# Rotary halves of the second pair: a swap by transfers inside SBUF in place of a product with a sign matrix

## The chip, the cores and the metric

The kernel runs on one core of one Trainium2 chip. The metric is device time in microseconds (us) of one execution, and what stands for a kernel is the median of its runs. Before the change the runs gave a median of 1918.45 us (1917.8 to 1918.78, three runs).

## What is computed

Two blocks of two layers each, in fp32, on 512 tokens of width 1024. The first block ("first pair" of layers below) has windowed attention, a Fourier mix and a short convolution. The second block ("second pair") is the one that the change touches. Each of its layers has three kinds of attention side by side (a: 6 heads with a dilated mixture, b: 4 heads of differential attention, c: 6 heads with latent queries and keys), a projection, a layer norm and a gated feed-forward part. The change is in kind c:

```python
q = (rms_norm(c_q, q_norm_g) @ w_uq).reshape(Bn, S, C_HEADS, C_NOPE + C_ROPE)     # 6 heads, 64 + 32
kv = (rms_norm(c_kv, kv_norm_g) @ w_ukv).reshape(Bn, S, C_HEADS, C_NOPE + C_V)
q_c = concat([q[..., :C_NOPE], apply_rope(q[..., C_NOPE:])])
k_c = concat([kv[..., :C_NOPE], broadcast(apply_rope(k_r))])                      # one rotary k for all heads

def apply_rope(x):                      # half = 16, angles of S = 512 positions
    x1, x2 = x[..., :half], x[..., half:]
    return concat([x1 * cos - x2 * sin, x2 * cos + x1 * sin])
```

So each group of 32 rotary values needs its own two halves of 16 swapped, one of them with its sign turned.

## The kernel before, in words

*Layout.* Activations stand with features on the 128 partitions and the 512 tokens along the row. `qr` holds the rotary part: `qr[:, 0, :]` the queries of heads 0 to 3 (4 x 32 partitions), `qr[0:64, 1, :]` those of heads 4 and 5, and `qr[64:96, 1, :]` the common rotary key. A swap of halves is then a swap of neighbouring blocks of 16 partitions. The kernel gets it from TensorE: `rot` is a 128x128 matrix of 0, 1 and -1, and `rot` times `qr` is the swapped and signed copy, in PSUM (`turn_rope`, line 1947). In the first pair the kernel does the same swap in another way: SyncE issues 16 transfers from SBUF to SBUF per layer, each of 16 partitions (lines 696 to 701), and the sign is in the table `sin1`.

*Weights.* Every weight tile comes into one of three slots of `raw` by a transfer that SyncE issues in the order of the list `stream`; it waits until GpSimd has finished with the tile that was three places ahead (line 708, 744). ScalarE copies it to `w_hi` (line 847), GpSimd subtracts to get `w_lo` (line 775), and TensorE makes three products for each one (`mm3`, lines 1411 to 1413). `w_hi` and `w_lo` have two slots. In a layer of the second pair the order of tiles is c, bq, bk, bv, a, av, up, then the four tiles of the output projection ("o",0,0), ("o",0,1), ("o",1,0), ("o",1,1), then the feed-forward tiles.

*The stretch of the change*, once in each layer l, y = 2 + l. Each engine follows an order written out by hand, and engines wait for each other by semaphores.

- TensorE: the av projection with eight early scores of kind b among it; then from the tile up: two groups of `qr` (lines 1945, 1946), three products for the key part `kn` with the two products of `rot` behind the second and the third one (line 1963), three for `qn`, two scores of kind b (units 8 and 9), four products for `vc`; then score(10), the first of kind c (line 1999), and the loop of the attention stage (from line 2001) with scores, transposes and products with the values. A score of kind c waits for `s_roped`, for the rotary key, and for the last `qn` copy (lines 1907 to 1909).
- ScalarE copies each result out of PSUM: the rotary key (line 1302), `qr` (line 1306, with the query scale in it), `kn` and `qn` (line 1311), `vc` (line 1315), then the exponentials (line 1290).
- VectorE, when the early scores are done, for both groups (lines 2623 to 2630): a product with `sin2` into `tmp_c`, a product with `cos2` in `qr`, and for each of the six heads the sum into `qc`. Behind that stand the first `scored` steps of the attention stage (line 2599).
- GpSimd, when the second group's product with `cos2` is done: the sum for the key of head 0 into `kc` (line 820) and five copies of it (line 823).
- SyncE has at this place the wait and the load for tile ("o",1,0).

PSUM banks: the two products of `rot` use banks 5 and 7 (`ROTB`), and the next user of each waits for the sums of its group (`emptied`). `tmp_c` lies in the same memory as the attention output `ao`; it is free in this stretch.

Of the kernel before, what the change touches and what calls it, by code (L numbers as in the profile page):

```python
# [16 lines left out]
ALU = mybir.AluOpType  # L17
# [3 lines left out]
P = 128  # L21
D = 1024
KD = D // P
SEQ, CTX, DEPTH = 512, 256, 2
# [19 lines left out]
QC = HD + ROPE  # L44
# [27 lines left out]
def _constants():  # L72

    f = np.float32
    c = {}
    c["ident"] = np.eye(P, dtype=f)
    pos = np.arange(SEQ)
    inv = np.power(f(10000.0), -np.arange(16, dtype=f) / f(16)).astype(f)
    ang = np.stack([(pos // 64).astype(f)[:, None] * inv, (pos % 64).astype(f)[:, None] * inv], 1)
    rows = np.arange(P)  # L80
    axis, freq = (rows % 64) // 32, rows % 16
    c["cos1"] = np.ascontiguousarray(np.cos(ang)[:, axis, freq].T.astype(f))
    sign = np.where(rows % 32 < 16, -1.0, 1.0).astype(f)[:, None]
    c["sin1"] = np.ascontiguousarray(np.sin(ang)[:, axis, freq].T.astype(f) * sign)

    def rotation(n, half):
        r = np.zeros((n, n), f)
        for i in range(n):
            first = (i % (2 * half)) < half
            r[i + half if first else i - half, i] = -1.0 if first else 1.0  # L90
        return r

    c["rot"] = rotation(P, 16)
    inv2 = np.power(f(10000.0), -np.arange(16, dtype=f) / f(16)).astype(f)
    ang2 = pos.astype(f)[:, None] * inv2
    c["cos2"] = np.ascontiguousarray(np.tile(np.cos(ang2).T, (P // 16, 1)).astype(f))
    c["sin2"] = np.ascontiguousarray(np.tile(np.sin(ang2).T, (P // 16, 1)).astype(f))
    q, k = np.arange(P)[:, None], np.arange(3 * P)[None, :] - P
    band = np.where(np.abs(q - k) <= P, 0.0, FAR).astype(f)
    c["band_mid"] = np.concatenate([np.zeros((P, CTX), f), band], 1)  # L100
    c["band_first"] = np.concatenate([np.zeros((P, CTX), f), band[:, P:]], 1)
    for n in (SEQ, CTX):
        t = np.outer(np.arange(n), np.arange(n)) % n * (2 * np.pi / n)
        c[f"dft{n}"] = np.concatenate([np.cos(t)[:, 0:n // 2 + 1], np.sin(t)[:, 1:n // 2]], 1).astype(f) / f(np.sqrt(n))
    t = np.outer(np.arange(HD), np.arange(HD)) % HD * (2 * np.pi / HD)
    two = np.eye(2)
    c["dft_ccos"] = np.kron(two, np.cos(t) / 8.0).astype(f)
    c["dft_csin"] = np.kron(two, -np.sin(t) / 8.0).astype(f)
    dist = SEQ - 1 - np.arange(SEQ + P)
    df = np.maximum(dist, 1).astype(f)  # L110
    large = 16 + (np.log(df / f(16)) / f(np.log(2048 / 16)) * f(16)).astype(np.int32)
    bucket = np.where(dist < 16, np.maximum(dist, 0), np.minimum(large, BUCKETS - 1))
    hot = np.zeros((BUCKETS + 2, SEQ + P), f)
    hot[bucket, np.arange(SEQ + P)] = (dist >= 0)
    times = (dist <= P).astype(int) + (dist % 4 == 0) + (dist % 16 == 0)
    ok = dist >= 0
    hot[BUCKETS] = np.where(ok & (times > 0), np.log(np.maximum(times, 1)), -FAR)
    hot[BUCKETS + 1] = np.where(ok, 0.0, -FAR)
    c["hot"] = hot
    pick = np.zeros((2, A_HEADS + B_HEADS), f)  # L120
    pick[0, :A_HEADS] = 1.0
    pick[1, A_HEADS:] = 1.0
    c["pick"] = pick
    fold = np.zeros((P, 2), f)
    for g in range(4):
        fold[32 * g:32 * g + 2] = np.eye(2, dtype=f)
    c["fold"] = fold
    d2 = 384 + np.arange(P)[:, None] - np.arange(SEQ)[None, :]
    c["causal"] = np.where(d2 >= 0, 0.0, FAR).astype(f)
    init = [0.8 - 0.6 * np.exp(-0.3 * l) for l in range(DEPTH)]  # L130
    c["lam_init"] = np.array([[-i, 1.0 - i] for i in init], f)
    return c


def _program(nc, I, out, seen):
    ctx = ExitStack()
    with ctx:
# [23 lines left out]
        rot = put("rot", [P, P])  # L161
# [84 lines left out]
        qr = at("qr", [P, 2, SEQ], names["g_hi"][0] + 4 * C_HEADS * SEQ)  # L246
# [3 lines left out]
        tmp_c = at("tmp_c", [P, 2, SEQ], ao2_at)  # L250
# [14 lines left out]
        sin2 = put("sin2", [P, SEQ])  # L265
# [26 lines left out]
        ps = ctx.enter_context(nc.psum_tensor("ps", [P, 8, 512], F32))  # L292
# [57 lines left out]
        s_proj = Signal(nc, ctx, seen, "proj")  # L350
# [9 lines left out]
        s_row_stored = Signal(nc, ctx, seen, "row_stored")  # L360
        s_sum_cols = Signal(nc, ctx, seen, "sum_cols")
        s_roped = Signal(nc, ctx, seen, "roped")
        s_rot = Signal(nc, ctx, seen, "rot")
        s_rot_in = Signal(nc, ctx, seen, "rot_in")
        s_rr = Signal(nc, ctx, seen, "rr")
        s_rr_mm = Signal(nc, ctx, seen, "rr_mm")
        s_scored = Signal(nc, ctx, seen, "scored")
# [6 lines left out]
        s_silu = Signal(nc, ctx, seen, "silu")  # L374
        s_ssq = Signal(nc, ctx, seen, "ssq")
        s_stored = Signal(nc, ctx, seen, "stored")
        s_strips = Signal(nc, ctx, seen, "strips")
        s_strips_b = Signal(nc, ctx, seen, "strips_b")
        s_causal = Signal(nc, ctx, seen, "causal")
# [116 lines left out]
        for l in range(DEPTH):  # L496
            outs = [((l, "out", ch, kh), [square(I["w_out"][l], ch, kh)], True) for ch, kh in ((0, 1), (0, 0), (1, 0), (1, 1))]
            mix = mix_tiles(l)
            if l == 0:
                first = [mod_tile(0, j) for _, _, j in FIRST]  # L500
# [157 lines left out]
        BB = {"bq": (1, 3), "bk": (5, 7)}  # L658
        CB = {"kn": (6, 1, 3), "qn": (0, 4, 6)}
        VCB = (2, 1, 3, 5)  # L660
        ROTB = (5, 7)
        TURNED = {}
        for step in range(STEPS):
            if turns(step) is not None:
# [28 lines left out]
        @block.sync  # L693
        def _(sp):
            for n, (what, loads, _) in enumerate(stream):
                if what[1:] == ("zc",):
                    sp.wait_ge(s_proj.sem, s_proj.at((what[0], ("kv",), 0, 0)))
                    for part, a, e in ((0, 0, 2), (1, 2, 5)):
                        for to in range(0, P, 16):
                            own = to ^ 16  # L700
                            sp.dma_start(swap[part][to:to + 16, :, :], qk[own:own + 16, a:e, 0:SEQ]).then_inc(s_swapped[part].sem, s_swapped[part].nth(what[0], 16))
# [27 lines left out]
                if what in ((1, "q", 0), (DEPTH, "c", 0)):  # L729
# [3 lines left out]
                    sp.wait_ge(s_scores.sem, s_scores.at((l, len(units1(l)) - 1)))  # L733
                    for s in range(2 - l):
                        sp.dma_start(gate_b[:, s, :], gate_rows[l, s].partition_broadcast(P)).then_inc(s_gate_b[s].sem, s_gate_b[s].nth(l, 16))
                if what == (DEPTH, "c", 0):
                    sp.wait_ge(s_row_stored.sem, s_row_stored.at(7))
                    sp.dma_start(rot[:], I["rot"]).then_inc(s_rot_in.sem, s_rot_in.nth(0, 16))
                if what == (1, "q", 1):
                    sp.wait_ge(s_scores.sem, s_scores.at((0, len(units1(0)) - 1)))  # L740
                    for dst, src in ((cos1[:], I["cos1"]), (sin1[:], I["sin1"])):
# [645 lines left out]
        def _(pe):  # L1387

            emptied = {b: s_ones.after(0) for b in range(8)}
# [446 lines left out]
            for l in range(DEPTH):  # L1836
                y = DEPTH + l
# [45 lines left out]
                for j in range(3):  # L1883
                    w = begin((y, "a", j))
                    for c in range(2):
                        i = 2 * j + c
# [57 lines left out]

                for g, n in ((0, P), (1, HD)):
                    up_q(4 * g, P * g, n, ("qr", g)).then_inc(s_mm.sem, s_mm.nth((y, "qr", g)))
                def turn_rope(g, n):

                    pe.wait_ge(*emptied[ROTB[g]])
                    emptied[ROTB[g]] = s_roped.after((y, g))  # L1950
                    pe.wait_ge(s_proj.sem, s_proj.at((y, "qr", g)))
                    pe.wait_ge(s_rot_in.sem, s_rot_in.at(0))
                    pe.matmul(ps[0:n, ROTB[g], :], rot[0:n, 0:n], qr[0:n, g, :], start=True, stop=True).then_inc(s_rot.sem, s_rot.nth((y, g)))

                for c in range(3):
                    b = CB["kn"][c]
                    pe.wait_ge(*emptied[b])
                    emptied[b] = s_proj.after((y, "kn", c, 1))
                    need((y, "up"), 2 * C_HEADS * QC + C_HEADS * HD)
                    mm3(ps[:, b, :], both_parts(ukv, lambda r: r[:, P * c:P * c + P]), both_parts(CKV, lambda r: r[:]),  # L1960
                        True, True).then_inc(s_mm.sem, s_mm.nth((y, "kn", c)))
                    if c > 0:
                        turn_rope(*((0, P), (1, QC))[c - 1])
                for c in range(3):
                    up_q(CB["qn"][c], C_HEADS * ROPE + P * c, P, ("qn", c, 1)).then_inc(s_mm.sem, s_mm.nth((y, "qn", c)))
                for i in range(EARLY, EARLY + 2):
# [34 lines left out]
                for step in range(FROM, STEPS):  # L2001
                    if EARLY + N_S <= step < len(UNITS):
                        score(step)
                    r = turns(step)
                    if r is not None:
                        i, b = RANKS[r], TURNED["unit", r]
# [112 lines left out]
        def _(dve):  # L2119
            V = nc.vector  # L2120

            def step(ins):

                ins.then_inc(s_dve_step.sem, s_dve_step.nth("latest"))
                dve.wait_ge(s_dve_step.sem, s_dve_step.count)
# [430 lines left out]
            for l in range(DEPTH):  # L2556
# [64 lines left out]
                    pair(2 * (i - 4) + 1)  # L2621
                R = slice(HD, QC)
                for g, n in ((0, P), (1, QC)):
                    dve.wait_ge(s_rot.sem, s_rot.at((y, g)))
                    step(V.tensor_tensor(tmp_c[0:n, g, :], ps[0:n, ROTB[g], :], sin2[0:n, :], ALU.mult))
                    V.tensor_tensor(qr[0:n, g, :], qr[0:n, g, :], cos2[0:n, :], ALU.mult).then_inc(s_kr_parts.sem, s_kr_parts.nth(y))
                    dve.wait_ge(s_kr_parts.sem, s_kr_parts.count)
                    for h in range(4 * g, 4 if g == 0 else C_HEADS):
                        own = slice(32 * (h % 4), 32 * (h % 4) + 32)
                        V.tensor_tensor(qc[R, h, :], qr[own, g, :], tmp_c[own, g, :], ALU.add).then_inc(s_roped.sem, s_roped.nth((y, g)))  # L2630
# [153 lines left out]
```

## Time and profile before

| | |
|---|---|
| median of the runs | 1918.45 us |
| the profiled execution | 1916.83 us |
| its span, first to last instruction | 1914.6 us |
| mean granted TensorE clock | 0.993 |
| TensorE (PE) busy | 1874.1 us, 98% |
| VectorE (DVE) busy | 797.1 us, 42% |
| ScalarE (ACT) busy | 821.3 us, 43% |
| GpSimd (POOL) busy | 710.0 us, 37% |
| DMA engines | 28.6% on SyncE's queue, 2.1% on ScalarE's |

Matmuls overlap in their pipeline, so a row's duration is longer than its step to the next row; for TensorE it is the starts that are to be compared. An fp32 product (both operands fp32, as with `rot`) goes through TensorE in two passes and stands as x2 in one row; the three products of `mm3` take one pass each. A number in square brackets behind a row is the engine's idle time before it and what ended it; a releaser is inferred by the profile from semaphores, so it is to be compared with the waits that the code has. A SyncE row (SPq) is the time that an issue takes on SyncE; the landing is given apart.

### The profile page before, as it was taken

How to read it: one execution, taken by the hardware profiler on the slowest of the kernel's cores; microseconds unless marked ns; L12 is line 12 of the kernel's file. 1: busy time of each engine (PE TensorE's matmuls, PEld its weight loads, DVE VectorE, ACT ScalarE, POOL GpSimd, SP SyncE). 2: the span in 40 equal slices, each digit the busy share in tenths (PEclk: the TensorE clock that was granted, in tenths of full speed). 3: DMA queues.
4: the chain of work that ended last, by engine and by line, in shares of the span. 5: the costliest groups of instructions: out<-in, count | busy, mean ns of one | idle time of the engine just before them, and what ended most of it. 6: DMA issues, size and time to landing. Idle time of an engine off the chain costs nothing.

```text
span 1914.6 us, 26609 instructions
## 1 busy us (share of the span) xinstructions
PE 1874.1 (98%) x10298; PEld 1600.6 (84%) x10298; DVE 797.1 (42%) x1802; ACT 821.3 (43%) x1576; POOL 710.0 (37%) x567
## 2 busy tenths in 40 slices
PE   7999999999999999999999999999999999999997
PEld 4888889878889888888988888888888898888886
DVE  4675576168355372775411110047277541111003
ACT  4221378373267464773332222226487333232212
POOL 2432322236522344203444454444420344445452
PEclk7999999999999999999999999999999999999999
DMA  9354431214412124202233323223320222332321
GB/s 341 132 181 131 123 67 50 73 45 138 154 27 72 62 93 129 73 12 89 80 96 89 110 88 132 88 80 103 119 83 2 89 88 88 95 103 88 132 88 44
DMA packets 198315, 185.60 MB, mean 97 GB/s; under 512 B 27246, under 2 KB 165636, under 8 KB 198192
## 3 DMA queue, kind: packets, MB, share of 16 engines
q1 hardware_dynamic: 183640, 172.52, 28.6%
q10 hardware_dynamic: 14552, 11.40, 2.1%
q8 instruction: 83, 1.36, 0.3%
q14 instruction: 40, 0.33, 0.1%
HBM read 179.11 MB, written 5.44 MB: 96 GB/s over the span
## 4 chain that ended last, share of the span: by engine, by line
PE 89%; ACT 4%; DVE 3%; issue 2%; POOL 2%; DMA 1%; ACTq 0%; DVEq 0%; SPq 0%
PE ps L1411 24%; PE ps L1413 24%; PE ps L1412 24%; PE ps L1996 3%; PE ps L1912 3%; PE ps L1504 3%; POOL w_lo L775 2%; PE ps L1471 2%; PE ps L2014 2%; PE ps L1490 1%; PE ps L1432 1%; ACT w_hi L847 1%; DMA res<-in_x 0%; ACT pt L908 0%; DMA raw<-in_w_in 0%
## 5 line engine op out<-in xcount | busy, mean ns | idle before, releaser
L775 POOL TENSOR_TENSOR w_lo<-raw,w_hi 128x512 fp32r<-128x512 f32 (+2 forms) x509 | 669.0, 1346 | 1083.1 <-ACT w_hi L847 1083.0
L847 ACT ACTIVATE w_hi<-raw 128x1024 fp32r<-128x1024 f32 (+1 forms) x257 | 254.1, 1034 | 242.2 <-PE ps L1413 190.9
L1411 PE MATMUL ps<-g_hi,w_lo 128*128 128x512 f32 (+1 forms) x928 | 348.4, 375 | 1.4 <-POOL w_lo L775 1.4
L1412 PE MATMUL ps<-g_lo,w_hi 128*128 128x512 f32 (+1 forms) x928 | 347.5, 374 | 0.0
L1413 PE MATMUL ps<-g_hi,w_hi 128*128 128x512 f32 (+1 forms) x928 | 347.4, 374 | 0.0
L1411 PEld LDWEIGHTS ps<-g_hi,w_lo 128*128 128x128 f32 x928 | 174.7, 188 | 34.0 <-issue 1.7
L1413 PEld LDWEIGHTS ps<-g_hi,w_hi 128*128 128x128 f32 x928 | 174.7, 188 | 31.1
L1412 PEld LDWEIGHTS ps<-g_lo,w_hi 128*128 128x128 f32 x928 | 174.7, 188 | 30.9
L2739 DVE TENSOR_TENSOR tmp_f<-ps,tmp_f 128x512 f32<-128x512 f32 x44 | 30.4, 692 | 370.7 <-PE ps L1413 370.7
L1411 PE MATMUL ps<-h_hi,w_lo 128*128 128x512 f32 (+1 forms) x496 | 177.5, 358 | 2.8 <-DVE h_lo L2134 2.3
L1412 PE MATMUL ps<-h_lo,w_hi 128*128 128x512 f32 (+1 forms) x496 | 175.4, 354 | 0.0
L1413 PE MATMUL ps<-h_hi,w_hi 128*128 128x512 f32 (+1 forms) x496 | 175.2, 353 | 0.0
L1411 PE MATMUL ps<-w_hi,hid_lo 128*128 128x512 f32 x352 | 137.1, 390 | 0.0
L1413 PE MATMUL ps<-w_hi,hid_hi 128*128 128x512 f32 x352 | 136.9, 389 | 0.0
L1412 PE MATMUL ps<-w_lo,hid_hi 128*128 128x512 f32 x352 | 136.9, 389 | 0.0
L1366 ACT ACTIVATE hid_hi<-tmp_f 128x512 fp32r<-128x512 f32 x44 | 27.8, 632 | 237.2 <-DVE tmp_f L2739 237.2
L2697 DVE SCALAR_TENSOR_TENSOR res<-res,ps 128x512 f32<-128x512 f32 x32 | 21.8, 684 | 231.6 <-PE ps L1413 231.3
L1411 PE MATMUL ps<-w_hi,g_lo 128*128 128x512 f32 (+3 forms) x320 | 114.2, 357 | 1.5 <-POOL w_lo L775 1.5
L1413 PE MATMUL ps<-w_hi,g_hi 128*128 128x512 f32 (+3 forms) x320 | 112.0, 350 | 0.0
L1412 PE MATMUL ps<-w_lo,g_hi 128*128 128x512 f32 (+3 forms) x320 | 111.8, 349 | 0.0
L1411 PEld LDWEIGHTS ps<-h_hi,w_lo 128*128 128x128 f32 x496 | 94.4, 190 | 20.3 <-issue 7.1
L1413 PEld LDWEIGHTS ps<-h_hi,w_hi 128*128 128x128 f32 x496 | 94.3, 190 | 13.0
(291 smaller groups left out, 3377.1 us busy)
## 6 DMA issues: line engine op xcount, KB each, us to landing
raw<-in_w_in SPq DMA_DIRECT2D x34, 1024.0 KB, 5.0
raw<-in_w_mod SPq DMA_DIRECT2D x24, 1024.0 KB, 6.4
raw<-in_w_gate SPq DMA_DIRECT2D x44, 512.0 KB, 3.7
raw<-in_w_up SPq DMA_DIRECT2D x44, 512.0 KB, 4.8
raw<-in_w_down SPq DMA_DIRECT2D x22, 1024.0 KB, 4.8
raw<-in_w_out SPq DMA_DIRECT2D x8, 1024.0 KB, 5.2
strips<-bias_rows ACTq DMA_DIRECT2D x18, 256.0 KB, 3.4
raw<-in_w_o SPq DMA_DIRECT2D x4, 1024.0 KB, 4.8
```

Source lines behind the costliest of these rows:

```text
L775: pool.tensor_tensor(w_lo[:, i % SPLIT, a:e], raw_of(what)[:, a:e], w_hi[:, i % SPLIT, a:e].bitcast(F32), ALU.subtract).then_inc(s_tile_lo ...
L847: act.activation(w_hi[:, i % SPLIT, a:b], raw_of(what)[:, a:b], ACT.Copy).then_inc(s_tile_hi.sem, s_tile_hi.nth((what, n)))
L1366: act.activation(hid_hi[:, j, :], tmp_f[:, 2 + j % 2, :], ACT.Copy).then_inc(s_hi.sem, s_hi.nth((y, "f", j)))
L1411: pe.matmul(o, lhs[1], rhs[0], start=first, stop=False)
L1412: pe.matmul(o, lhs[0], rhs[1], start=False, stop=False)
L1413: return pe.matmul(o, lhs[0], rhs[0], start=False, stop=last)
L1471: m = pe.matmul(ps_flat[:, o0 + CTX + col:o0 + CTX + col + k.shape[1]], q, k, start=j == 0, stop=j == len(products) - 1)
L1504: m = pe.matmul(ps_flat[:, o0:o0 + HD], turned, v, start=j == 0, stop=j == n - 1)
L1912: pe.matmul(ps[:, b, 0:u["n"]], u["q"], u["k"], start=True, stop=True).then_inc(s_scores.sem, s_scores.nth((y, i)))
L1996: m = pe.matmul(ps[:, b, 0:HD], pt2[r % N_P][:, P * j:P * j + P], v, start=j == 0, stop=j == len(u["vs"]) - 1)
L2014: m = pe.transpose(ps[:, b, P * j:P * j + P], probs_of(i)[:, P * j:P * j + P], ident[:])
L2739: V.tensor_tensor(tmp_f[:, 2 + j % 2, :], ps[:, 2 * ((j + 2) % 4) + 1, :], tmp_f[:, j % 2, :], ALU.mult).then_inc(s_glu.sem, s_glu.nth((y, ...
```

## The change

The matrix `rot`, its load and its two semaphores go, and with them the two TensorE products per layer. In their place SyncE issues eight transfers per layer from `qr` to `tmp_c`, each of 16 partitions and from the neighbouring block (`to ^ 16`): six with both groups (64 KB) and, for partitions 96 to 127, two with group 0 alone (32 KB). They stand in `stream` in front of the load of tile ("o",1,0), behind a wait for ScalarE's copy of the second group of `qr`. VectorE waits for all eight, in both groups, and multiplies `tmp_c` by `sin2` in place; the sign is in the table now. The order of all other instructions is the same.

```diff
-    c["rot"] = rotation(P, 16)
-    c["sin2"] = np.ascontiguousarray(np.tile(np.sin(ang2).T, (P // 16, 1)).astype(f))
+    c["sin2"] = np.ascontiguousarray(np.tile(np.sin(ang2).T, (P // 16, 1)).astype(f) * np.where(rows % 32 < 16, -1.0, 1.0).astype(f)[:, None])
...
         @block.sync
             for n, (what, loads, _) in enumerate(stream):
+                if what[1:] == ("o", 1, 0):
+                    sp.wait_ge(s_proj.sem, s_proj.at((what[0], "qr", 1)))
+                    for to in range(0, P, 16):
+                        own, g = to ^ 16, 2 if to < QC else 1
+                        sp.dma_start(tmp_c[to:to + 16, 0:g, :], qr[own:own + 16, 0:g, :]).then_inc(s_rope_in.sem, s_rope_in.nth(what[0], 16))
...
-                if what == (DEPTH, "c", 0):
-                    sp.wait_ge(s_row_stored.sem, s_row_stored.at(7))
-                    sp.dma_start(rot[:], I["rot"]).then_inc(s_rot_in.sem, s_rot_in.nth(0, 16))
...
-                def turn_rope(g, n):
-
-                    pe.wait_ge(*emptied[ROTB[g]])
-                    emptied[ROTB[g]] = s_roped.after((y, g))
-                    pe.wait_ge(s_proj.sem, s_proj.at((y, "qr", g)))
-                    pe.wait_ge(s_rot_in.sem, s_rot_in.at(0))
-                    pe.matmul(ps[0:n, ROTB[g], :], rot[0:n, 0:n], qr[0:n, g, :], start=True, stop=True).then_inc(s_rot.sem, s_rot.nth((y, g)))
-
...
-                    if c > 0:
-                        turn_rope(*((0, P), (1, QC))[c - 1])
...
                 for g, n in ((0, P), (1, QC)):
-                    dve.wait_ge(s_rot.sem, s_rot.at((y, g)))
-                    step(V.tensor_tensor(tmp_c[0:n, g, :], ps[0:n, ROTB[g], :], sin2[0:n, :], ALU.mult))
+                    dve.wait_ge(s_rope_in.sem, s_rope_in.at(y))
+                    step(V.tensor_tensor(tmp_c[0:n, g, :], tmp_c[0:n, g, :], sin2[0:n, :], ALU.mult))
```

## Rows read from the trace of the kernel before

**Rows 1.** The page, part 4: the chain that ended last, by engine.
```profile
PE 89%; ACT 4%; DVE 3%; issue 2%; POOL 2%; DMA 1%; ACTq 0%; DVEq 0%; SPq 0%
```
**Rows 2.** Timeline of VectorE, layer 2: start, duration, engine, line, tiles, [idle <- releaser].
```profile
1398.58 0.69 DVE L2625 TENSOR_TENSOR tmp_c<-ps,sin 128x512 f32<-128x512 f32 x1 [4.88 <-PE ps L1953]
```
**Rows 3.** Timeline of TensorE in layer 1, 762 to 800.
```profile
776.28 0.39 PE L1413 MATMUL ps<-ckv_hi,w_hi 128*128 128x512 f32 x1
776.51 1.02 PE L1953 MATMUL ps<-qr,rot 128*128 128x512 f32 x2
776.96 0.80 PE L1411 MATMUL ps<-ckv_hi,w_lo 128*128 128x512 f32 x1
777.60 0.40 PE L1412 MATMUL ps<-ckv_lo,w_hi 128*128 128x512 f32 x1
...
785.20 0.33 PE L1412 MATMUL ps<-w_lo,ckv_hi 128*128 128x384 f32 x1
785.38 0.34 PE L1413 MATMUL ps<-w_hi,ckv_hi 128*128 128x384 f32 x1
785.80 1.10 PE L1912 MATMUL ps<-kc,qc 96*128 96x512 f32 x2
```
**Rows 4.** Timeline of VectorE in layer 1, 765 to 800.
```profile
777.56 0.69 DVE L2625 TENSOR_TENSOR tmp_c<-ps,sin 128x512 f32<-128x512 f32 x1 [4.88 <-PE ps L1953]
778.29 0.69 DVE L2626 TENSOR_TENSOR qr<-qr,cos 128x512 f32<-128x512 f32 x1
...
783.32 2.37 DVE L2630 TENSOR_TENSOR qc<-qr,tmp_c 32x512 f32<-32x512 f32 x2
```
**Rows 5.** Waits of TensorE's weight loads, 770 to 800: us in total, times, longest.
```profile
PEld ps L1912 <- ACT vc L1315: 0.4, 1, 0.4
```
**Rows 6.** Windows: length, busy (instructions) by engine, granted clock, DMA share, GB/s.
```profile
777.00:781.00 4.00, 4.00 (x17) 2.74 (x16) 3.31 (x5) 3.13 (x6) 0.00 (x0) 1.00 0.00 0
...
786.00:790.00 4.00, 3.75 (x26) 2.86 (x25) 2.96 (x10) 3.69 (x11) 2.39 (x5) 1.00 0.00 0
...
786.00:880.00 94.00, 92.63 (x648) 77.81 (x648) 70.78 (x284) 72.84 (x221) 11.88 (x12) 1.00 0.13 40
```
**Rows 7.** Timeline of ScalarE: second `qr` copy; a weight tile behind the stage.
```profile
775.33 0.59 ACT L1306 ACTIVATE qr<-ps 64x512 f32<-64x512 f32 x1 [0.78 <-PE ps L1413]
...
874.37 1.99 ACT L847 ACTIVATE w_hi<-raw 128x1024 fp32r<-128x1024 f32 x2
```
**Rows 8.** Timeline of SyncE's issues, 770 to 773.
```profile
770.17 2.16 SPq L744 DMA_DIRECT2D raw<-in_w_o  x2
```
**Rows 9.** Timeline of SyncE's issues: swaps of the first pair, layer 2 (narrow windows).
```profile
450.66 0.60 SPq L701 DMA_DIRECT2D swap<-qk  x1
...
455.76 0.60 SPq L701 DMA_DIRECT2D swap<-qk  x1
```
**Rows 10.** DMA issues, KB each, us to landing: at 450.7, at 456.0, and at the end.
```profile
swap<-qk SPq DMA_DIRECT2D x1, 64.0 KB, 3.7
...
swap<-qk SPq DMA_DIRECT2D x1, 96.0 KB, 2.7
...
y<-res SPq DMA_DIRECT2D x2, 256.0 KB, 2.0
```
**Rows 11.** Timeline of SyncE's issues, 36 to 40: loads of plain rows, back to back.
```profile
36.81 0.43 SPq L711 DMA_DIRECT2D band_mid<-in_band_mid  x1
37.29 0.43 SPq L711 DMA_DIRECT2D band_first<-in_band_first  x1
```
**Rows 12.** Timeline of TensorE, 35 to 41: its longest wait.
```profile
40.25 1.11 PE L1566 MATMUL ps<-ident,xn 128*128 128x128 f32 x4 [4.36 <-ACT tmp_x L959]
```
**Rows 13.** Windows around that wait, columns as in rows 6.
```profile
38.00:40.00 2.00, 0.00 (x0) 0.00 (x0) 0.00 (x0) 2.00 (x4) 0.00 (x0) 0.50 1.07 408
...
44.00:46.00 2.00, 2.00 (x5) 1.54 (x6) 1.34 (x3) 0.00 (x0) 2.00 (x2) 0.50 0.83 228
46.00:48.00 2.00, 2.00 (x11) 1.88 (x10) 0.00 (x0) 0.00 (x0) 2.00 (x4) 0.56 0.80 308
```

More of the change, by code:

```diff
@@ L84, in _constants @@
     c["sin1"] = np.ascontiguousarray(np.sin(ang)[:, axis, freq].T.astype(f) * sign)
[L86 to L91, printed above, removed]
-    c["rot"] = rotation(P, 16)
     inv2 = np.power(f(10000.0), -np.arange(16, dtype=f) / f(16)).astype(f)
@@ L362, in _program @@
         s_roped = Signal(nc, ctx, seen, "roped")
-        s_rot = Signal(nc, ctx, seen, "rot")
-        s_rot_in = Signal(nc, ctx, seen, "rot_in")
         s_rr = Signal(nc, ctx, seen, "rr")
@@ L376, in _program @@
         s_stored = Signal(nc, ctx, seen, "stored")
+        s_rope_in = Signal(nc, ctx, seen, "rope_in")
         s_strips = Signal(nc, ctx, seen, "strips")
@@ L660, in _program @@
         VCB = (2, 1, 3, 5)
-        ROTB = (5, 7)
         TURNED = {}
```

## The prediction

> **What bounds the kernel now.** I read the page's chain first: TensorE carries 89% of what ended last [rows 1], so what TensorE loses or gains in a stretch reaches the end, unless it waits there for something else. The change touches one short stretch in each of the two layers of the second pair, so I then read the timelines of that stretch, engine by engine. Layer 2 repeats layer 1: its first rotary product on VectorE stands at 1398.58, behind the same wait of 4.88 us, against 777.56 [rows 2, 4]. All times below are those of layer 1.
>
> TensorE multiplies without a stop up to the last vc matmul at 785.38. Those matmuls start 0.17 apart, so the next instruction, the first score that reads rotary halves (score(10), line 1912), could start at 785.55; it starts at 785.80 [rows 3]. VectorE stands still for 4.88 us until the first sign-matrix product is there, and then works from 777.56 to 783.32 + 2.37 = 785.69 [rows 4]. In the code, score(10) waits for the last of these additions (`s_roped` of group 1, line 1907), and it starts 0.11 us behind it. The view of waits puts the 0.4 us on ScalarE's copy of vc [rows 5], which ends at nearly the same moment; but no wait in front of score(10) names that copy. That is the reading on which all else rests: **the rotary chain on VectorE and the matmuls on TensorE end within 0.25 us of each other**. VectorE's chain has no slack, and what makes it start later delays TensorE by as much.
>
> Behind that point TensorE is busy 92.63 of 94.00 us in the attention stage [rows 6]. VectorE's first work on scores comes straight behind the chain, and ScalarE's exponentials wait for that, so all three engines start the stage from one moment, and a late start isn't caught up.
>
> **The change part by part.**
>
> *Removed from TensorE.* Two fp32 products per layer, in two passes each. The first starts at 776.51. Without it, the kn matmul behind it would start then, and the next one 0.23 later (the step from 776.28 to 776.51), at 776.74, where now it starts at 777.60 [rows 3]: 0.86 us. The second product is of the same size: 1.72 us per layer, and TensorE would reach score(10) at 785.55 - 1.72 = 783.83. It gains nothing by that while it waits for VectorE. Also gone is the fourth vc matmul's wait for bank 5, whose release came long before, so at no gain.
>
> *Removed from SyncE.* One load of the sign matrix and the wait in front of it, between the two pairs. The load behind it is of a tile that ScalarE takes much later, at the end of the pair; nothing.
>
> *Arithmetic on VectorE.* The twelve instructions per layer stay. One kind reads the swapped halves from SBUF in place of PSUM; the product with both operands in SBUF takes the same 0.69 us as the one out of PSUM [rows 4]. The sign sits in the table at no cost. The chain keeps its 785.69 - 777.56 = 8.13 us. GpSimd's sum for k starts on VectorE's last cosine product and moves with it, so the slow additions beside it (2.37 us for two) stay as they are, and before that GpSimd is idle.
>
> *Added on SyncE: when the transfers can start.* They wait for ScalarE's copy of the second group, which ends at 775.33 + 0.59 = 775.92 [rows 7]. SyncE is free: its last issue before is the load that the transfers are put ahead of (w_o, tile "o",1,0), at 770.17 [rows 8]. That load would go out some 11 us later; ScalarE splits the tile in front of it at 874.37 only [rows 7], so what is queued behind SyncE's new wait pays nothing, and its megabyte isn't in front of anything. First issue, some hundredths behind the copy: 775.95.
>
> *Their price.* The kernel has such transfers in its first pair, 16 partitions and 64 or 96 KB each, swapped by 16. The eighth of sixteen is issued at 450.66 and the last at 455.76 [rows 9]: (455.76 - 450.66)/8 = 0.64 us apart. The eighth lands 3.7 us later with a 1 MB load in front, the last after 2.7 [rows 10]. Here no other transfer runs (DMA 0.00 from 777 to 781 [rows 6]), so I take 2.65 for the last one of 32 KB. It is issued at 775.95 + 7 x 0.64 = 780.43 and lands at 783.08; VectorE starts at 783.11, **5.55 us later than now**. Bounds: the pieces moved here are contiguous in a partition, those of the first pair were not on the side that is read. Back-to-back loads of plain rows are issued 0.48 apart [rows 11], which gives 775.95 + 3.36 + 2.65 = 781.96 and a start 4.45 later; the shortest landing in the kernel, 2.0 [rows 10], takes off another 0.65: 3.8. With the loaded landing of 3.7 it is 6.6. I take the middle one, since its row is the same form of transfer.
>
> The Trainium skill ("DMA: Bandwidth & Descriptors", section "Rules for kernel authors") has it that transfers under 64 KB cost mostly overhead and should be merged into one, which speaks against this change, as the rows do. The same page of the Trainium skill ("Issuing engines are not separate DMA queues") calls the time to initiate a DMA usually small beside the DMA itself; the rows differ (eight issues take 5.1 us, a landing 2.7), and by that sentence the sum would be that of the rival "issue is cheap" below.
>
> *What TensorE's idle time brings.* It reaches score(10) at 783.83 and gets it at 785.80 + 5.55 = 791.35: 7.5 us idle. Early in the kernel TensorE waits 4.36 us, until 40.25 [rows 12]. The granted clock is down to 0.50 (1.2 GHz) before that gap ends, still 0.50 in 44 to 46 and 0.56 in 46 to 48 [rows 13], so back at 1.00 (2.4 GHz) at about 47.8: 7.6 us behind the restart, in the last 3.8 of which TensorE is fully busy. A gap of 7.5 us should do the same. The stage that starts here is dense from its first microseconds (3.75 of 4 [rows 6]), so it is like the stretch from 44 on: 3.8 us at half clock, of which half, **1.9 us**, is lost. Bounds: nothing, and 7.6/2 = 3.8.
>
> *Sum.* Per layer 5.55 + 1.9 = 7.45; two layers 14.9. Against the profiled execution of 1916.83 us that is 1931.7. The median of the runs, 1918.45, is 1.6 above that execution, so I forecast **1933.3 us**, 0.8% slower.
>
> **The rivals.**
>
> *Cheaper issue (chance 0.24).* Contiguous pieces go out 0.48 apart, a start 4.45 later. With a clock loss of 0 to 1.9: 2 x 4.45 = 8.9 to 2 x 6.35 = 12.7, so 1927.3 to 1931.2, middle 1929.2. For it: SyncE's time for an issue differs by form. Against: all rows of this form have 0.64.
>
> *Dearer landing and clock (0.10).* 6.6 + 3.8 = 10.4 per layer: 1939.3. For it: the loaded landing, and all of the early restart. Against: the queues are empty and the stage is dense.
>
> *Issue is cheap (0.05).* All transfers are under way at once and the last lands 2.7 us after 775.95; VectorE starts at 778.65, 1.1 late, TensorE idles 3.1 us, with a clock loss between 0 and 1.9: 1920.7 to 1924.5, middle 1922.6. Against: the swap rows.
>
> *TensorE keeps what it is spared (0.03), the side of faster.* If score(10) finds its operands ready, each layer gains 1.72 + 0.25 = 1.97: 1914.5 in all. It decides at one point: VectorE's chain must end by 783.83, so start by 775.70, before ScalarE has even made the copy (775.92). That can only be if the reading of score(10)'s wait is wrong and ScalarE's vc copy releases it. The view of waits says so by name [rows 5]; the code doesn't.
>
> *No effect (0.02).* The stage's 1.4 us without matmuls and what TensorE is spared absorb the delay: about 1918.
>
> **How the numbers follow.** A measurement tells some 0.2%, 3.8 us, from no change: 1914.6 to 1922.3. The forecast, with 1930 to 1937 as its own range, has 0.56. Slower: 0.56 + 0.24 + 0.10 + 0.04 of "issue is cheap" = 0.94. Same: 0.02 and the last 0.01 of "issue is cheap". Faster: 0.03. The range, 1926.5 to 1939.5, takes in the forecast, the cheaper issue and the dear case; that leaves 0.10 outside, and some of the ends of each.
>
> **What would show it.** The profile after should have VectorE idle about 10.4 us in front of its first rotary product, released by a DMA; eight issues on SyncE 0.64 apart from 775.9; a gap of about 7.5 us on TensorE in front of score(10); and a granted clock of 0.5 in the gap and some 4 us behind it. From score(10) to the end of the stage it should take longer by the clock's part alone. I am wrong if score(10) starts before VectorE's last addition, if the stage catches the delay up, or if the clock stays at 1.00 over the gap.

## The result

The changed kernel takes 1938.64 us (median of 4 runs, 1937.79 to 1940.14), the kernel before 1918.12 us beside it (4 runs). The ratio is 1.0111, 95% interval 1.0098 to 1.0124: slower by 20.5 us. The forecast was 1933.3 in a range of 1926.5 to 1939.5. The direction and the path were as forecast. The loss of 20.5 us is larger than the 14.9 of the sum: the clock's term was far too low, and the term of the late start a little too high.

| | before | after |
|---|---|---|
| profiled execution | 1916.83 us | 1937.79 us |
| its span | 1914.6 us | 1935.5 us |
| mean granted clock | 0.993 | 0.984 |
| TensorE busy | 1874.1 us | 1884.1 us |

TensorE is busy 10 us longer with less work to do, and the mean clock is lower. Line numbers after are lower by 8 (up to SyncE's part and in TensorE's helpers) to 18 (VectorE's part).

The chain that ended last, in order of time, in the changed stretch of layer 1 after the change (start, duration, engine and line):

```profile
775.26 0.60 ACT qr L1298
775.86 0.02 issue
775.87 0.59 SPq L690
776.46 0.04 issue
776.50 0.59 SPq L690
...
779.66 0.59 SPq L690
780.25 0.04 issue
780.29 1.96 DMA tmp_c<-qr
782.25 0.02 issue
782.27 0.70 DVE tmp_c L2607
```

So the path goes ScalarE's copy, SyncE's issues 0.63 apart, one landing, VectorE. Seven issues stand on it; the eighth starts at 780.29, and its landing is counted from that start, 1.96 us. From the first issue to VectorE it takes 782.27 - 775.87 = 6.40 us. The chain passes from ScalarE to VectorE without TensorE here. VectorE's timeline after, to be held against [rows 4]:

```profile
782.27 0.69 DVE L2607 TENSOR_TENSOR tmp_c<-tmp_c,sin 128x512 f32<-128x512 f32 x1 [9.67 <-DMA tmp_c<-qr]
783.00 0.69 DVE L2608 TENSOR_TENSOR qr<-qr,cos 128x512 f32<-128x512 f32 x1
...
788.03 2.35 DVE L2612 TENSOR_TENSOR qc<-qr,tmp_c 32x512 f32<-32x512 f32 x2
```

The idle time before the first product is 9.67 in place of 4.88, and the chain itself is as long as it was: 788.03 + 2.35 - 782.27 = 8.11 us. TensorE's timeline after, to be held against [rows 3]; the first row is the first product on the tile up:

```profile
772.29 0.39 PE L1403 MATMUL ps<-cq_hi,w_lo 128*128 128x512 f32 x1
...
782.16 0.50 PE L1904 MATMUL ps<-bk,bq 128*128 128x512 f32 x1 [0.58 <-ACT qc L1303]
...
784.41 0.34 PE L1405 MATMUL ps<-w_hi,ckv_hi 128*128 128x384 f32 x1
790.48 2.04 PE L1904 MATMUL ps<-kc,qc 96*128 96x512 f32 x2 [5.74 <-DVE qc L2612]
...
883.54 0.48 PE L1403 MATMUL ps<-w_hi,g_lo 128*128 128x512 f32 x1
```

And the two rows of before at the ends of the same stretch, first product on the tile up and first product of the output projection:

```profile
772.36 0.39 PE L1411 MATMUL ps<-cq_hi,w_lo 128*128 128x512 f32 x1
...
873.05 0.48 PE L1411 MATMUL ps<-w_hi,g_lo 128*128 128x512 f32 x1
```

From these the loss can be split. From the first product on the tile up to score(10) it takes 785.80 - 772.36 = 13.44 us before and 790.48 - 772.29 = 18.19 after: **4.75 us for the late start**. From score(10) to the output projection, with the same instructions on every engine, it takes 873.05 - 785.80 = 87.25 before and 883.54 - 790.48 = 93.06 after: **5.81 us in a stage that the change doesn't touch**. Layer 2 has 4.74 and 5.80. Twice 10.56 is 21.1, and the two profiled executions differ by 1937.79 - 1916.83 = 20.96, so next to nothing is left over.

The second part is the clock. Windows after, columns as in [rows 6]:

```profile
784.00:786.00 2.00, 0.75 (x5) 0.42 (x3) 1.91 (x4) 1.23 (x3) 0.00 (x0) 1.00 0.81 304
786.00:788.00 2.00, 0.00 (x0) 0.00 (x0) 1.93 (x3) 0.00 (x0) 0.00 (x0) 0.68 0.00 0
788.00:790.00 2.00, 0.00 (x0) 0.00 (x0) 1.94 (x2) 0.00 (x0) 1.86 (x2) 0.50 0.00 0
...
796.00:798.00 2.00, 2.00 (x12) 2.00 (x12) 1.06 (x9) 0.86 (x4) 0.00 (x0) 0.50 0.00 0
...
802.00:804.00 2.00, 2.00 (x11) 1.71 (x10) 0.98 (x4) 1.22 (x4) 0.00 (x0) 0.55 0.43 114
804.00:806.00 2.00, 2.00 (x14) 1.49 (x13) 0.57 (x3) 0.85 (x3) 0.00 (x0) 1.00 0.21 45
```

The clock falls to 0.50 (1.2 GHz) at about 786.7, some 2 us into the gap, and is back at 1.00 (2.4 GHz) at about 803.8, 13.3 us behind TensorE's restart, though TensorE shows as busy 2.00 of 2 us all the while. The busy share by itself doesn't tell how fast TensorE works. Layer 2, with a gap of 5.71 us up to 1422.01, differs in the fall and not in the return:

```profile
1420.00:1422.00 2.00, 0.00 (x0) 0.02 (x1) 1.94 (x3) 0.00 (x0) 1.94 (x2) 0.90 0.00 0
...
1434.00:1436.00 2.00, 2.00 (x13) 1.71 (x12) 1.39 (x6) 1.15 (x5) 0.00 (x0) 0.69 0.50 131
```

There the clock falls at about 1421.6, only 0.4 us in front of the restart, and is back at about 1435.3, again 13.3 us behind it. The loss is the same, so what counts here is the low stretch behind the restart, not the one in the gap.

### The profile page after: what moved, and what is told of

Its sections match the earlier page's. It is cut to its first block, busy times and chain, and to the rows that moved or that the text cites. A ratio compares the mean times of both kernels' runs of the same rounds, so it can differ in the third digit from the quotient of the medians.

```text
span 1935.5 us, 26604 instructions
## 1 busy us (share of the span) xinstructions
PE 1884.1 (97%) x10290; PEld 1609.8 (83%) x10290; DVE 797.9 (41%) x1802; ACT 821.8 (42%) x1576; POOL 709.7 (37%) x567
## 4 chain that ended last, share of the span: by engine, by line
PE 88%; DVE 3%; ACT 3%; issue 2%; POOL 2%; DMA 1%; SPq 0%; ACTq 0%; DVEq 0%
PE ps L1403 24%; PE ps L1404 24%; PE ps L1405 24%; PE ps L1978 3%; PE ps L1904 3%; PE ps L1496 3%; PE ps L1996 2%; POOL w_lo L767 2%; PE ps L1463 2%; PE ps L1482 2%; PE ps L1424 1%; ACT w_hi L839 1%; DVE qc L2612 1%; DMA res<-in_x 0%; SPq L690 0%
## 5 line engine op out<-in xcount | busy, mean ns | idle before, releaser
L1405 PEld LDWEIGHTS ps<-h_hi,w_hi 128*128 128x128 f32 x496 | 94.3, 190 | 12.9
```

The lines of the kernel that those rows point to most:

```text
L1405: return pe.matmul(o, lhs[0], rhs[0], start=False, stop=last)
```

## The experiments

Eight experiments, each run beside the kernel before; the last is the changed kernel once more. Two lengths are read off each trace in the same way as above: L, from the first product on the tile up to score(10), and S, from score(10) to the first product of the output projection. They are layer 1's; where S differs by 0.2 us or more in layer 2, both are given. One execution of each was profiled.

| kernel | L, us | S, us | median, us | granted clock in the stretch of layer 1 |
|---|---|---|---|---|
| before | 13.44 | 87.25 | 1918.12 | 1.00 |
| changed | 18.19 | 93.06 | 1938.64 | low until 13.3 us behind the restart |
| e1_filler | 18.21 | 87.25, 87.53 | 1927.06 | 1.00 |
| e2_two_transfers | 15.92 | 88.32 | 1930.89 | low until 3.9 us behind |
| e3_no_swap | 12.33 | 87.20 | 1914.93 | 1.00 |
| e4_fourteen | 21.98 | 88.66, 88.92 | 1937.82 | low until 4.1 us behind, 4.7 in layer 2 |
| e5_filler_behind | 18.18 | 93.42, 93.21 (with useless work) | 1939.57 | low until 5.3 us behind, 4.8 in layer 2 |
| e6_two_queues | 16.49 | 87.33 | 1927.46 | low only from 785.2 to 788.7, before score(10) |
| e7_products_earlier | 13.21 | 87.18 | 1918.45 | 1.00 |
| e8_changed_again | 18.21 | 92.86 | 1937.75 | low until some 13 us behind |

The kernel before stood at 1917.3 us beside e1 to e4 (13 runs, 1916.67 to 1918.78) and at 1919.5 beside e5 to e8, on another chip (17 runs, 1916.01 to 1924.2); each ratio below is against its own. The scatter of the second group is to be kept in mind, as nothing was changed in it.

**e1_filler: is the second half of the loss the clock?**

```diff
+                pe.wait_ge(*emptied[7])
+                for _ in range(24):
+                    pe.matmul(ps[:, 7, :], ckv_hi[:, 0:P], ckv_hi[:], start=True, stop=True)
                 for i in range(EARLY + 2, EARLY + N_S):
                     score(i)
```

> The changed kernel with 24 matmuls of 512 columns (ckv_hi by ckv_hi, into bank 7, which nobody reads) put in front of score(10), to keep TensorE busy in its 5.7 us gap. The late start of the rotary chain stays as it is (score(10) some 4.7 us later than before, per layer), so the two parts of the loss come apart. Theory (a late start of 4.75 us and a low clock of 5.8 us per layer): the clock stays at 1.00, and the kernel takes 2 x 4.75 = 9.5 us more than before, 1927.6, some 11 us less than the changed one. Rival (the attention stage itself became slower, by its order of waits or by contention, and the clock is only a companion): the time stays near 1938 although the clock is 1.00.

1927.06 us (1925.42 to 1928.42), ratio 1.0049 (1.0032 to 1.0066). TensorE in front of score(10):

```profile
786.04 5.64 PE L1983 MATMUL ps<-ckv_hi 128*128 128x512 f32 x24
791.91 1.10 PE L1904 MATMUL ps<-kc,qc 96*128 96x512 f32 x2 [0.23 <-DVE qc L2615]
```

The late start is the same to 0.02 us (18.21), the clock is 1.00 in every window of the stretch in both layers, and S is back at 87.25 and 87.53. The kernel with 48 more products is 11 us faster than the changed one. Against 1917.3, 9.8 us remain, and the late start is 2 x 4.77 = 9.5. The rival, a stage that is slow for another reason, falls: behind the filler the program is that of the changed kernel, and the clock is what differs.

**e2_two_transfers: issue or landing?**

```diff
-                    for to in range(0, P, 16):
-                        own, g = to ^ 16, 2 if to < QC else 1
-                        sp.dma_start(tmp_c[to:to + 16, 0:g, :], qr[own:own + 16, 0:g, :])...
+                    for a, e, g in ((0, QC, 2), (QC, P, 1)):
+                        sp.dma_start(tmp_c[a:e, 0:g, :], qr[a:e, 0:g, :])...
```

> The changed kernel with the same bytes moved by two transfers per layer (96 partitions with both groups, 32 with group 0) in place of eight; the halves are not swapped, a part of the computation that is left out here. Theory (SyncE's eight issues at 0.64 us each are what makes the chain late): six issues fewer take 3.8 us off the start of VectorE's chain; it starts about 1 us later than in the kernel before, and TensorE's gap in front of score(10) is some 2 us. If the clock doesn't fall in so short a gap, 2 x 1.0 = +2 us against before: 1920; if it falls as in the changed kernel, up to 1932. Rival (the landing of transfers inside SBUF is what is slow): VectorE starts as late as with eight, 1938.

1930.89 us (1923.53 to 1932.83), ratio 1.0064 (1.0042 to 1.0085). The timelines of SyncE, VectorE and TensorE:

```profile
775.57 1.24 SPq L689 DMA_DIRECT2D tmp_c<-qr  x2
...
779.70 0.69 DVE L2606 TENSOR_TENSOR tmp_c<-tmp_c,sin 128x512 f32<-128x512 f32 x1 [7.39 <-DMA tmp_c<-qr]
...
787.91 1.55 PE L1903 MATMUL ps<-kc,qc 96*128 96x512 f32 x2 [3.42 <-DVE qc L2611]
```

From the first issue to VectorE's start it takes 4.13 us (779.70 - 775.57), in the changed kernel 6.40. Six issues fewer would be 3.8 by the step; 2.27 came off, since the larger transfers land later (779.70 less the second issue's start at about 776.2 is 3.5, against 2.0). So the issues are the larger part of the 6.40 (seven steps are 4.4), but merging them buys less than the theory's 3.8: of the 4.75 us of late start, 15.92 - 13.44 = 2.48 stay with two transfers.

The clock falls even with a gap of 3.42 us, in layer 1 0.5 us behind its end (788.4 to 791.8 at 0.50), and costs S 1.1 us per layer. That is the profiled execution, the one of 1923.53. With the start alone all four would be near 1917.3 + 2 x 2.5 = 1922.3, but the other three took 1929.03, 1932.76 and 1932.83, at mean clocks of 0.987 and 0.986 against 0.990. The kernel before kept within 2.1 us beside them, so these three lost some 7 to 10 us by something that the transfers bring in. A longer low stretch behind the gap is the likely cause, but no trace of them was kept, and the mean clock can't settle it: it takes in the start of the kernel too, its first 51 us, of which the profiled executions spend between 20 us (before) and 31 us (e3) at 0.50.

**e3_no_swap: what is the removal worth?**

```diff
-                if what[1:] == ("o", 1, 0):
-                    ... (the wait and the eight transfers)
...
-                    dve.wait_ge(s_rope_in.sem, s_rope_in.at(y))
+                    dve.wait_ge(s_proj.sem, s_proj.at((y, "qr", g)))
```

> The changed kernel without its transfers: VectorE waits for ScalarE's copy of each group and multiplies what stands in tmp_c; the swap of the halves is left out of the computation. It shows what the removal of TensorE's two products is worth by itself. Theory (TensorE gets 1.72 us per layer back, less what it waits for ScalarE's qn copies, 0.58, in front of score(9)): score(10) starts about 1.15 us earlier than before, 2.3 us in all, 1915.8. Rival (the chain on VectorE is no bound, TensorE's own work is, in full): 3.9 us less, 1914.2. Rival (nothing is gained, since ScalarE's vc copy releases score(10)): 1918.

1914.93 us (10 runs), ratio 0.9987 (0.9977 to 0.9996): 2.4 us less; L is 12.33, 1.11 less than before. This is the theory, 1.15 per layer. Of the 1.72 us of TensorE's two products 0.58 go to the wait for ScalarE's qn copies in front of score(9), a wait that the products had hidden. In this kernel 2.4 us is all that a swap at no cost could bring.

**e4_fourteen: does a longer gap cost more clock?**

```diff
-                        own, g = to ^ 16, 2 if to < QC else 1
-                        sp.dma_start(tmp_c[to:to + 16, 0:g, :], qr[own:own + 16, 0:g, :])...
+                        own = to ^ 16
+                        for g in range(2 if to < QC else 1):
+                            sp.dma_start(tmp_c[to:to + 16, g, :], qr[own:own + 16, g, :])...
```

> The changed kernel with each group moved by a transfer of its own: fourteen per layer in place of eight, the same bytes. It doubles neither wait nor arithmetic, it only makes the gap longer by six issues, 6 x 0.64 = 3.8 us per layer. Theory (every issue delays all that follows by its full time, and the clock's loss depends on the stage behind the gap, not on the gap's length): +7.7 us against the changed kernel, 1946.3. Rival (the clock's loss grows with the gap, as when 5.7 us idle cost more than 4.36 did early in the kernel): more than that, 1950 or above.

1937.82 us (1936.66 to 1947.2), ratio 1.0118 (1.0094 to 1.0141): no slower than with eight. Both theories missed the time, and the trace says why. The late start grew exactly as forecast, L = 21.98, that is 3.79 more than with eight (six issues of 0.63). But S is 88.66 in place of 93.06, and 88.92 in layer 2 in place of 93.05; the two all but cancel, 7.6 us more and 8.5 less. Score(10) in TensorE's timeline:

```profile
795.22 2.04 PE L1905 MATMUL ps<-kc,qc 96*128 96x512 f32 x2 [9.48 <-DVE qc L2613]
```

And the windows behind it, columns as in [rows 6]:

```profile
796.00:798.00 2.00, 2.00 (x7) 1.18 (x6) 1.05 (x3) 0.70 (x2) 1.82 (x4) 0.50 0.00 0
798.00:800.00 2.00, 2.00 (x14) 1.76 (x12) 0.56 (x5) 1.85 (x6) 0.00 (x0) 0.67 0.00 0
800.00:802.00 2.00, 2.00 (x21) 2.00 (x19) 1.93 (x10) 1.68 (x6) 0.00 (x0) 1.00 0.00 0
```

Here the clock is back at about 799.3, 4.1 us behind the restart (4.7 in layer 2), where it took 13.3 us in the changed kernel with the same instructions behind the gap, and this after a gap of 9.48 us in place of 5.74. So the kind of work behind the gap doesn't set by itself how long the clock stays low, and a longer gap doesn't mean a longer low stretch behind it: 3.9 us behind a gap of 3.42, 13.3 behind 5.74, 4.1 behind 9.48. One of the four executions took 1947.2, within 1 us of the expected 1946.3; it has no trace.

**e5_filler_behind: wide products behind the restart.**

```diff
                 for i in range(EARLY + 2, EARLY + N_S):
                     score(i)
+                pe.wait_ge(*emptied[7])
+                for _ in range(16):
+                    pe.matmul(ps[:, 7, :], ckv_hi[:, 0:P], ckv_hi[:], start=True, stop=True)
```

> The changed kernel with 16 matmuls of 512 columns (ckv_hi by ckv_hi, into bank 7, read by nobody) put directly behind score(10), so behind the gap and not in it. In the changed kernel the clock came back 13.3 us after TensorE's restart in both layers, with fourteen transfers 4.2 us after it, with the same work behind. At half clock the 16 matmuls take 6.8 us, at full clock 3.4. Theory (the stage's own small fp32 products are too thin to bring the clock back reliably, wide matmuls without a wait do): the clock is back within some 7 us of the restart in each layer; of the 2 x 5.8 us loss about 2 x 2 to 2 x 3 remain, and 2 x 3.4 to 6.8 us of useless work come on top: about 1937 to 1941, with little scatter. Rival (it is the moment of the restart alone that decides, whatever work follows): low stretches of 4 and of 13 us stand beside each other as before, and the time is 1936 to 1950 with a wide scatter.

1939.57 us (1938.82 to 1942.93), ratio 1.0111 (1.0098 to 1.0124). TensorE's timeline in layer 1:

```profile
791.85 2.05 PE L1904 MATMUL ps<-kc,qc 96*128 96x512 f32 x2 [5.68 <-DVE qc L2615]
792.91 6.21 PE L1985 MATMUL ps<-ckv_hi 128*128 128x512 f32 x16
```

And one of its windows, columns as in [rows 6]:

```profile
796.00:798.00 2.00, 2.00 (x8) 1.58 (x7) 0.00 (x0) 0.00 (x0) 0.00 (x0) 0.72 0.00 0
```

The clock is back at about 797.1, 5.3 us behind the restart, and 4.8 us behind it in layer 2. The filler lasts 798.96 - 792.91 = 6.05 us and costs about what it saves: S is 93.42, against 93.06 without it. The times are those that the theory expected, and no stretch of 13 us is left. But only one execution was profiled, and in e4 the clock was back after 4.1 us without any filler, so it isn't shown that the wide products brought it back.

**e6_two_queues: half the issues on ScalarE's queue.**

```diff
-                    for to in range(0, P, 16):
+                    for to in (0, 16, 32, 48):
...
+                for to in (64, 80, 96, 112):
+                    own, g = to ^ 16, 2 if to < QC else 1
+                    if to == 64:
+                        act.wait_ge(s_proj.sem, s_proj.at((y, "qr", 1)))
+                    act.dma_start(tmp_c[to:to + 16, 0:g, :], qr[own:own + 16, 0:g, :])...
                 for what, dst, scale in (("kn", kc, 1.0), ("qn", qc, -QC ** -0.5)):
```

> The changed kernel with four of the eight transfers issued by ScalarE's queue, right behind its copies of qr, the other four by SyncE as before. Theory (the issues in a row on one queue are what is late): the last issue is some 2.5 us earlier, VectorE's chain starts some 2.3 us later than before the change in place of 4.8, TensorE's gap is 3.3 us in place of 5.7; 2 x 2.3 = +4.6 us by the start alone, plus a clock loss between 0 and 2 x 5.8: 1922 to 1934. Rival (transfers from two queues get in each other's way, or the issues hold ScalarE's kn copies up): no earlier start, 1938.

1927.46 us (1923.36 to 1929.19), ratio 1.0042 (1.003 to 1.0054): of the change's loss 8.0 us are left. The timelines of ScalarE, VectorE and TensorE:

```profile
776.47 2.78 ACTq L1304 DMA_DIRECT2D tmp_c<-qr  x4
779.30 3.69 ACT L1309 ACTIVATE kc<-ps 64x512 f32<-64x512 f32 x6 [2.86 <-PE ps L1411]
...
781.04 0.69 DVE L2614 TENSOR_TENSOR tmp_c<-tmp_c,sin 128x512 f32<-128x512 f32 x1 [7.84 <-DMA tmp_c<-qr]
...
784.27 0.50 PE L1910 MATMUL ps<-bk,bq 128*128 128x512 f32 x1 [2.06 <-ACT qc L1309]
785.50 0.79 PE L1910 MATMUL ps<-bk,bq 128*128 128x512 f32 x1 [0.73 <-ACT qc L1309]
```

The theory was right in the main on VectorE: 1.8 us earlier than in the changed kernel, 3.0 later than before where 2.3 was expected. Part of the difference is the landing: 2.3 to 2.7 us here, against 2.0 to 2.3 on one queue in the changed kernel. It missed that the rival is right too: ScalarE copies nothing for 2.86 us while it issues, its kn and qn copies slip, and TensorE's one gap becomes several shorter ones (2.06 and 0.73 us in front of scores 8 and 9). The clock still falls, though no gap is longer than 2.06 us; columns as in [rows 6]:

```profile
784.00:786.00 2.00, 1.00 (x2) 0.68 (x3) 1.94 (x3) 1.93 (x4) 0.00 (x0) 0.81 0.00 0
786.00:788.00 2.00, 2.00 (x7) 1.90 (x7) 1.90 (x4) 1.15 (x3) 1.16 (x1) 0.50 0.00 0
```

Its low stretch, 785.2 to 788.7, lies in front of score(10). There it costs next to nothing, because VectorE's chain ends at 789.17 and score(10) starts at 789.37; S is 87.33, as before the change.

**e7_products_earlier: is it VectorE that releases score(10)?** The kernel before, with TensorE's two sign-matrix products put one place earlier, so that VectorE's chain starts earlier too.

```diff
-                    if c > 0:
-                        turn_rope(*((0, P), (1, QC))[c - 1])
+                    if c < 2:
+                        turn_rope(*((0, P), (1, QC))[c])
```

> The kernel before the change, with the sign-matrix products one place earlier: behind the first and the second kn product in place of the second and the third. Theory (VectorE's chain is the bound by 0.25 us in front of score(10)): the chain starts 0.7 us earlier, score(10) comes straight behind the vc matmuls, 2 x 0.25 = 0.5 us less than before, 1916.8. Rival (it is ScalarE's vc copy that releases score(10)): no change. The two are nearly too close for the time to tell; the start of score(10) in the trace tells them apart, at 0.25 against 0 behind the last vc matmul's step.

The timelines of TensorE and ScalarE in layer 1:

```profile
787.67 0.33 PE L1413 MATMUL ps<-w_hi,ckv_hi 128*128 128x384 f32 x1
787.84 1.02 PE L1912 MATMUL ps<-kc,qc 96*128 96x512 f32 x2
...
786.71 1.82 ACT L1315 ACTIVATE vc<-ps 128x384 f32<-128x384 f32 x4
```

Score(10) now starts 0.17 behind the last vc matmul, L is 13.21 (13.20 in layer 2), 0.23 less than before. With only the sign-matrix products and the chain behind them moved, the wait in front of score(10) is gone. ScalarE's four vc copies run from 786.71 to 788.53, 0.45 each, so at 787.84 only two of the four had ended; before the change the third ended at about 785.8, just as score(10) started. So it was VectorE's chain that released score(10), and the name that the view of waits gave, ScalarE's vc copy [rows 5], was a coincidence of two ends. The time, 1918.45 against 1919.5 us, ratio 0.9994 (0.9985 to 1.0002), fits the 0.5 us and doesn't prove it.

**e8_changed_again: the scatter.**

> The changed kernel again, unaltered, to see how its time scatters beside that of the others and in how many executions the clock stays low for long. Theory (the low stretch behind the restart is 13 us long when the restart falls badly and 4 when it falls well, at a price of 5.8 and 1.9 us per layer): times between 1927 + 4 = 1931 and 1927 + 12 = 1939, with a lower granted clock where the time is longer. Rival (for this kernel the low stretch always has the same length): all within 1 us of 1938.6.

Six executions of the changed kernel: 1932.35, 1935.88, 1936.49, 1939.01, 1939.20 and 1942.73 us, with mean clocks of 0.989, 0.987, 0.986, 0.985, 0.988 and 0.980; the ratio is 1.0096 (1.008 to 1.0112). The rival's spread of 1 us is far too small, and the theory's 1931 to 1939 is exceeded too. By and large the time is longer where the clock is lower, with 1939.20 as the exception. But this doesn't show low stretches of two lengths. The kernel before, which has no gap here, scatters from 1916.01 to 1924.2 us beside it, 8 us against 10. And the one execution with a trace, that of 1939.01, has 13 us behind the restart in both layers (S is 92.86 and 92.91), as the changed kernel had in its first trace. In all four stretches of this kernel that a trace shows, the clock was back 12.9 to 13.3 us behind the restart.

## Why the prediction was right, and where a term was off

*The reading of score(10)'s wait* was right, and e7 shows it. It was the step that could have turned the sign.

*TensorE's part removed.* 0.86 us per product: the last vc matmul starts 12.12 us behind the first product on the tile up in place of 13.02. That is 0.90 less in place of 1.72, since a wait that the products hid became visible (0.58 us for ScalarE's qn copies and the step up to it). The prediction said that TensorE would reach score(10) at 783.83; it was 784.58. It cost nothing, because the gap swallowed it, but it halves what TensorE's time was worth in the rival on the side of faster: e3 has 1.11 us per layer, 2.4 in all, not 3.9.

*The late start* was put at 5.55 us and is 4.75. The step between issues was right (0.63 against 0.64), and so was the release: first issue at 775.87. Off was the landing of the last one, 1.96 us in place of 2.65. The figure was taken from a transfer of 96 KB, and this one has 32; in the changed kernel 64 KB land after 2.3 us and 32 KB after 2.0. The other 0.1 is a start of this execution that is 0.07 earlier and the shorter step, seven times. With VectorE earlier than forecast and TensorE later (784.58), the gap was 5.74 us and not 7.5.

*The clock* was put at 1.9 us per layer, with 3.8 as its bound, and is 5.81. **This is the term that was mis-sized.** The step that failed is the one that took the low stretch of the early part, 3.8 us from the moment of full work [rows 13], as the length for this stage because TensorE is as busy here. It lasted 13.3 us in both layers. Half of 13.3 would be 6.65, so TensorE was the bound for most of it. In e4 the clock was back after 4.1 us, and S lost 1.4. The mechanism was right, e1 shows it by taking it away. But 5.81 lies outside the term's own bounds, and that the time still came within the range, 0.9 us below its upper end, is luck: that end was set by a start of 6.6 us, which didn't come, and that left room for a clock loss that the prediction had not allowed for. The rival "dearer landing and clock" had the right total, 10.4 per layer against 10.56, for half a right reason: the clock was dearer than its 3.8, and the landing was not dear at all.

*Nothing behind the wait on SyncE paid:* the load for ("o",1,0) went out at 780.93 and S shows no trace of it in e1 (87.25). *No catching up:* the loss of the start arrives in full, in e1 as 9.8 us where the traces have 2 x 4.77.

*What stays open* is why the clock stays low for 4 us behind the gap in one kernel and for 13 in another with the same instructions behind it. The traces of e2, e4 and the changed kernel show that it differs between kernels. That it differs between executions of one kernel is likely from the times of e2, and not shown. Whether the wide products of e5 shortened it is open, and the moment of the restart was not tried by itself.

## What to carry to other kernels

Price several transfers on a chain as the steps between their issues plus the last one's landing, counted from the start of its own issue: here seven steps of 0.63 us and a landing of 1.96, together 6.4 us, in place of two matmuls of 0.86 us. When an edit takes work from the busiest engine, look for the chain that ends at the same point; here TensorE already waited 0.25 us for it, so the freed time only made the gap longer. A new gap of some us on TensorE is to be charged twice, for itself and for the clock behind it. The second charge may be the larger, 1.1 us in e2, 1.4 to 1.7 in e4 and 5.8 in the changed kernel, and it didn't follow the length of the gap. Useless matmuls put into the gap bought it back (11 us here). None of the variants with transfers beats the kernel before.

## What the runs showed of the hardware

- The granted clock of TensorE fell to 0.50 in or right behind gaps of 3.42, 5.74 and 9.48 us, and was back 3.9, 13.3 and 4.1 us behind the restart. TensorE's busy share was 2.00 of 2 us from the restart on. In e6 it fell although the gaps were of 2.06 and 0.73 us with one matmul between them.
- The moment of the fall differs for one and the same gap: 2.0 us into it in layer 1 of the changed kernel and 5.3 in layer 2, with the same 13.3 us behind the restart.
- Transfers of one form inside SBUF landed after 2.3 us with 64 KB and 2.0 with 32 KB where no load was in front, against 3.7 for 64 KB behind a load of 1 MB [rows 10].
- Pieces that are contiguous in a partition were issued no faster (0.63 apart) than those of the first pair (0.64), so the rival of cheaper issue had no ground. Issues on ScalarE's queue took 0.61 each, with one of 0.84 in layer 1 (2.78 for four), and held its copies up.
- Kernels with the transfers differ by 2 to 11 us from one execution to the next. The kernel before, without a fall in this stretch, stays within 2 us of its median beside e1 to e4, but runs from 1916.0 to 1924.2 beside e5 to e8, so not all of that scatter is due to the change.
